# Delta rule: scores kept from the early stage, residual in device memory, seven steps a tile

## The chip, the cores and the metric

One core of a Trainium2 chip. The metric is the device time of one execution in microseconds (us); lower is better. TensorE (PE) multiplies matrices, VectorE (DVE), ScalarE (ACT) and GpSimd (POOL) work element by element, SyncE (SP) issues the transfers. Each engine takes its own instructions strictly in order and waits on semaphores.

## What is computed

Three blocks over 512 tokens of width 1024, each with a gated feed-forward part. The change lies in the third block's gated delta rule, eight heads of 128 by 128, and in what stands around it:

```python
def gated_delta_rule_chunked(q, k, v, g, beta):
    """S_t = exp(g_t)(I - b_t k_t k_t^T) S_{t-1} + b_t k_t v_t^T ; o_t = S_t^T q_t."""
    ...
    gamma = jnp.exp(jnp.where(tri, G[..., :, None] - G[..., None, :], -jnp.inf))
    kb = kc * bc[..., None]
    A = jnp.where(strict, jnp.einsum("bnhid,bnhjd->bnhij", kb, kc) * gamma, 0.0)
    T = lax.linalg.triangular_solve(A + eye, jnp.broadcast_to(eye, A.shape),
                                    left_side=True, lower=True)
    ...
    def step(state, inp):
        u_i, w_i, qg_i, kd_i, att_i, dl_i = inp
        v_new = u_i - jnp.einsum("bhcd,bhde->bhce", w_i, state)
        o = jnp.einsum("bhcd,bhde->bhce", qg_i, state) + jnp.einsum("bhij,bhje->bhie", att_i, v_new)
        state = state * dl_i[..., None, None] + jnp.einsum("bhcd,bhce->bhde", kd_i, v_new)
        return state, o
```

The output then goes through a norm, gates, the product with `w_out` (out2) and a residual sum with the block's input.

## The kernel before

All weights come as 333 units of 512 KB through a ring of six slots (`ring`); SP loads unit u once u-5 units are done. ScalarE rounds each unit to `whi` (L1130), VectorE takes the rest to `wlo` (L1789), and TensorE makes three products per pair (L382 to L384). Both splits run three units ahead.

The third block starts at unit `small2`; unit `dq` 0 is five units later. `XT`, the residual by tokens, lies in `arena` columns 0 to 7 from the norm before (`layered`, L1893) to the sum after out2 (L1842).

*Early stage*, in the units `gqkv` 17 to 21: for each of four tiles of 128 tokens and two groups g of four heads, TensorE spreads decays and beta, VectorE makes beta-scaled keys, TensorE the key products `akk`, and VectorE multiplies their four 32x32 diagonal blocks by the decay into `diag` (L2381). VectorE inverts all these blocks by substitution (L2368, L2370) beside the units `gatea`; the two last transposes (L2422, L2423) end it (`inverted`).

*Delta stage*, from 1679.98 us: `gdn_order` interleaves the two groups, group 1 `LAG` steps behind group 0, and every engine walks the same list of (tile c, group g, part). A tile has nine parts:

- 0: decays `gb` (L961, L962), beta spread `bb` and exp spread `ge` on TensorE; `gam` and `eg` on ScalarE; scaled keys `kb` on VectorE (L2462)
- 1: key products `kk`, value transposes `vt`; scores `at` = -`kk` x `gam` (L2466); ScalarE scales the values (`vb`, L1660); GpSimd makes `kbg` = `kb` x `eg` (L1768)
- 2 to 5: the 128x128 inverse from 32x32 blocks: x5, y5, x6, y6, each a product of TensorE that ScalarE or VectorE copies (x5, x6, y6 on ScalarE, t6 and y5 on VectorE, L2472 to L2474); beside them mean square of the last tile (`ms`, L1006), q products `kq`, key transposes `kt` (L1065), decayed query `eg` (`qg`, L2489)
- 6: `ks` = `kbg` x state; VectorE subtracts it from the values (`r`, L2494) and makes `kd` (L2499)
- 7: new values `vn`; ScalarE copies them into the buffer of `kb`
- 8: `o` (L1100, L1102) and the state product `s`; VectorE norms `o` (L2513) and updates the state (L2518)

GpSimd copies the inverse blocks of a tile into `u`, `t5` and `t6` in part 0 (L1760, L1763), after the tile before has made its new values, and adds the finished tile into the mix (L1773) in part 5. `claim(b)` makes TensorE wait until the last reader of bank b is done; group g uses banks 4g to 4g+3. Before the stage GpSimd clears these buffers with four memsets (L1747, L1748), and VectorE and ScalarE wait for them (`cleared`). In the last tile four pairs of out2 products on `whi` fill TensorE's waits.

## Time and profile before

| | us |
|---|---|
| median of 3 runs | 2209.91 |
| lowest, highest | 2207.5, 2213.14 |
| span of the profiled execution | 2206.0 |
| TensorE busy in it | 2151.8 (98%) |
| VectorE, ScalarE, GpSimd busy | 1299.3, 916.9, 91.5 |

The page gives the profiled execution's span, from its first to its last instruction; its own device time isn't listed apart. Busy time counts an engine's instructions, not its waits; a matmul's end is modelled, so the distance of two starts says more than the length. In a row of the order of time, a bracket gives the idle time before it and what ended it. Operations named L956 are all small products of the delta rule, told apart by shape and place.

### The profile page before, as it was taken

The numbers are of one execution on the slowest core, as the hardware profiler recorded it, in microseconds if no ns is written. First come the engines' busy times: TensorE is split into PE (matmuls) and PEld (weight loads), VectorE is DVE, ScalarE is ACT, GpSimd is POOL, SyncE is SP. The second block draws the span as 40 slices with busy tenths as digits, with TensorE's granted clock in tenths as the row PEclk, the third lists the DMA queues.
The fourth block names the chain that finished last, engine by engine and source line by source line (L and its number), as shares of the span: only waits on it lengthen the run. The fifth ranks groups of instructions, "written<-read, shape, count | busy, mean of one in ns | idle before, by whom it ended". The sixth has DMA issues, their size and how long they took to land.

```text
span 2206.0 us, 26933 instructions
## 1 busy us (share of the span) xinstructions
PE 2151.8 (98%) x10736; PEld 1744.8 (79%) x10736; DVE 1299.3 (59%) x1986; ACT 916.9 (42%) x1549; POOL 91.5 (4%) x123
## 2 busy tenths in 40 slices
...
GB/s 199 94 58 77 67 87 96 96 96 115 98 75 105 67 29 124 97 100 99 116 96 77 96 67 96 77 23 93 77 78 57 1 39 92 99 96 96 115 96 76
DMA packets 50667, 189.82 MB, mean 86 GB/s; under 512 B 5616, under 2 KB 5616, under 8 KB 49776
## 3 DMA queue, kind: packets, MB, share of 16 engines
...
## 4 chain that ended last, share of the span: by engine, by line
PE 89%; DVE 6%; ACT 2%; issue 1%; DMA 1%; POOL 0%; DVEq 0%; ACTq 0%; POOLq 0%
PE bank L382 26%; PE bank L384 26%; PE bank L383 26%; PE bank L956 2%; PE bank L682 1%; DMA ring<-stream 1%; DVE small L1815 1%; PE bank L512 1%; PE bank L660 1%; DVE arena L1842 1%; ACT whi L1130 1%; PE bank L597 0%; DVE arena L1932 0%; PE bank L671 0%; DVE arena L1861 0%
## 5 line engine op out<-in xcount | busy, mean ns | idle before, releaser
L382 PE MATMUL bank<-xs,whi 128*128 128x512 f32 (+2 forms) x1992 | 773.1, 388 | 10.2 <-DVE xs L2148 7.4
L384 PE MATMUL bank<-xs,wlo 128*128 128x512 f32 (+2 forms) x1992 | 753.4, 378 | 0.0
L383 PE MATMUL bank<-xs,whi 128*128 128x512 f32 (+2 forms) x1992 | 752.9, 378 | 0.0
L1789 DVE TENSOR_TENSOR wlo<-ring,whi 128x1024 fp32r<-128x1024 f32 x333 | 416.3, 1251 | 296.6 <-ACT whi L1130 296.2
L1130 ACT ACTIVATE whi<-ring 128x1024 fp32r<-128x1024 f32 x333 | 350.4, 1054 | 262.8 <-DMA ring<-stream 262.8
L382 PEld LDWEIGHTS bank<-xs,whi 128*128 128x128 f32 x1992 | 377.5, 190 | 93.3 <-issue 9.5
L384 PEld LDWEIGHTS bank<-xs,wlo 128*128 128x128 f32 x1992 | 376.8, 189 | 69.3
L383 PEld LDWEIGHTS bank<-xs,whi 128*128 128x128 f32 x1992 | 377.6, 190 | 68.0 <-issue 2.9
L382 PE MATMUL bank<-whi,xs 128*128 128x512 f32 (+1 forms) x808 | 315.2, 390 | 3.5 <-issue 2.0
L384 PE MATMUL bank<-whi,xs 128*128 128x512 f32 (+1 forms) x808 | 311.9, 386 | 0.0
L383 PE MATMUL bank<-wlo,xs 128*128 128x512 f32 (+1 forms) x808 | 311.8, 386 | 0.0
L1433 ACT ACTIVATE arena<-bank,par 128x512 f32<-128x512 f32 x132 | 103.0, 780 | 433.2 <-PE bank L384 433.2
L2091 DVE SCALAR_TENSOR_TENSOR arena<-bank,par,arena 128x511 f32<-128x511 f32 x132 | 98.9, 749 | 286.1 <-ACT arena L1433 286.1
L382 PEld LDWEIGHTS bank<-whi,xs 128*128 128x128 f32 x808 | 152.1, 188 | 38.2 <-issue 5.6
L384 PEld LDWEIGHTS bank<-whi,xs 128*128 128x128 f32 x808 | 152.0, 188 | 30.4
L383 PEld LDWEIGHTS bank<-wlo,xs 128*128 128x128 f32 x808 | 152.2, 188 | 29.9 <-issue 0.5
L2093 DVE SCALAR_TENSOR_TENSOR arena<-bank,par,arena 128x510 f32<-128x510 f32 x132 | 98.9, 749 | 4.7
L1932 DVE SCALAR_TENSOR_TENSOR arena<-bank,par,arena 128x511 f32<-128x511 f32 (+2 forms) x96 | 71.8, 748 | 45.6 <-ACT arena L1596 35.1
L1727 POOL TENSOR_TENSOR arena<-arena 128x512 f32<-128x512 f32 x32 | 52.2, 1668 | 492.0 <-PE bank L512 306.3
L1596 ACT ACTIVATE arena<-bank,par 128x512 f32<-128x512 f32 x24 | 16.5, 687 | 86.0 <-PE bank L384 86.0
L1949 DVE TENSOR_REDUCE small<-bank 128x1 f32<-128x128 f32 (+3 forms) x64 | 31.2, 487 | 34.3 <-PE bank L662 26.5
L2097 DVE TENSOR_TENSOR arena<-arena 128x512 f32<-128x512 f32 x66 | 48.4, 733 | 3.1 <-ACT arena L1436 1.0
...
## 6 DMA issues: line engine op xcount, KB each, us to landing
ring<-stream SPq DMA_DIRECT2D x333, 512.0 KB, 3.6
...
arena<-xt SPq DMA_DIRECT2D x4, 512.0 KB, 6.7
arena<-xn SPq DMA_DIRECT2D x1, 2048.0 KB, 7.9
out<-arena SPq DMA_DIRECT2D x4, 512.0 KB, 2.6
con<-consts SPq DMA_DIRECT2D x1, 744.0 KB, 11.8
arena<-brow SPq DMA_DIRECT2D x1, 512.0 KB, 12.3
...
```

Of the source, the lines that this page charges most:

```text
L382: nc.tensor.matmul(out, ah, bh, start=first, stop=False)
L383: nc.tensor.matmul(out, ah, bl, start=False, stop=False)
L384: return nc.tensor.matmul(out, al, bh, start=False, stop=last)
L956: m = nc.tensor.matmul(tile(b)[0:rows, hh, 0:n], l(hh), r(hh), start=True, stop=True)
L1130: A(whi[:, v % SLOTS, :], ring[:, v % SLOTS, :], ACT.Copy).then_inc(whi_done, 1)
L1433: A(acc[:, s, :], bank_of(up, j)[:], ACT.Identity, bias=col(cols, 4 * j + 3), scale=col(cols, 4 * j + 2)).then_inc(scalar_out, scalar_at.n ...
L1727: nc.gpsimd.tensor_tensor(XT[:, tt, h], XT[:, tt, h], GB[:, i, h], op).then_inc(gpsimd_out, gpsimd_at.next("gained" if i == 0 else "shifte ...
L1789: V.tensor_tensor(wlo[:, v % SLOTS, :], ring[:, v % SLOTS, :], whi[:, v % SLOTS, :], ALU.subtract).then_inc(wlo_done, 1)
L1932: STT(dst[:, shift:], u[:, 0:SEQ - shift], w, dst[:, shift:], ALU.mult, ALU.add).then_inc(vector_out, vector_at.next())
L2091: STT(acc[:, s, 1:], u[:, 0:SEQ - 1], col(cols, 4 * j + 1), acc[:, s, 1:], ALU.mult, ALU.add).then_inc(vector_out, vector_at.next())
L2093: STT(acc[:, s, 2:], u[:, 0:SEQ - 2], col(cols, 4 * j), acc[:, s, 2:], ALU.mult, ALU.add).then_inc(vector_out, vector_at.next("conv", l, j))
L2097: V.tensor_tensor(hid[:, p, :], sg[:, p % 2, :], acc[:, s, :], ALU.mult).then_inc(vector_out, vector_at.next("hidden", l, p))
```

## The change

The early stage keeps its decayed key products whole (`scores`, negated, all eight in `arena` columns 0 to 7), and GpSimd copies the diagonal blocks from them. The residual goes out to device memory (`kept`) ahead of the load of unit `dq` 0 and comes back ahead of the load of unit out2+6. In the delta stage `bb`, `kb`, `kk`, `at` and `kbg` are gone: x5 and x6 read `scores`, `ks` multiplies the plain keys, and `r` adds it times a negated column of beta times the decay, head by head. `t5`, `t6` and `u` are double and GpSimd places a tile's blocks a tile ahead, so there are eight memsets. A tile has seven parts, group 1 runs three behind.

```diff
@@ -183,6 +185,13 @@
...
+    if u == FIRST["dq"]:
+        sp.wait_ge(vector_out, vector_at.find("layered", TILES - 1))
+        sp.dma_start(kept, arena[:, 0:8, :]).then_inc(kept_sem, 16)
+    if u == FIRST["out2"] + SLOTS:
+        sp.wait_ge(kept_sem, 16)
+        sp.wait_ge(tensor_out, tensor_at.find("x6", (TILES - 1, 1)))
+        sp.dma_start(arena[:, 0:8, :], kept).then_inc(xn_sem, 16)
@@ -229,13 +238,17 @@
...
-G |= dict(zip(("at", "u", "kbg", "kd", "vb", "qq"), (heads(scratch[:, 8 * g + i, :]) for i in range(6))))
...
+G |= dict(zip(("kd", "vb", "qq"), (heads(scratch[:, 8 * g + 3 + i, :]) for i in range(3))))
+G["u"] = [heads(scratch[:, 8 * g + i, :]) for i in range(2)]
+pairs, more = scratch[:, 8 * g + 6:8 * g + 8, :].rearrange("p a n -> p (a n)"), scratch[:, 8 * g + 2, :]
+G["pairs"], G["more"] = pairs, more
+quarter = [pairs[:, 256 * i:256 * (i + 1)].rearrange("p (h n) -> p h n", h=4) for i in range(4)]
+half = [more[:, 256 * i:256 * (i + 1)].rearrange("p (h n) -> p h n", h=4) for i in range(2)]
+G["t6"], G["x5"], G["x6"], G["t5"] = [quarter[0], half[0]], quarter[1], quarter[2], [quarter[3], half[1]]
...
-LAG, STEPS = 4, 9
+LAG, STEPS = 3, 7
+scores = [heads(arena[:, i, :]) for i in range(2 * TILES)]
@@ -1010,85 +1023,71 @@
...
+        u, t5, t6 = G["u"][c % 2], G["t5"][c % 2], G["t6"][c % 2]
         if part == 0:
...
-            four(b + 1, lambda hh: spread_rows(2, 4 * g + hh), lambda hh: parts(2, 1)[0:72, cs]).then_inc(tensor_out, tensor_at.next("bb", t))
...
-        elif part == 1:
...
-            four(b + 1, lambda hh: gk[:, 4 * g + hh, cs], lambda hh: G["kb"][:, hh, :]).then_inc(tensor_out, tensor_at.next("kk", t))
...
+                m = nc.tensor.transpose(tile(b + 1)[:, hh, :], gv[:, 4 * g + hh, cs], ident)
...
-        elif part == 2:
...
-        elif part == 3:
...
+        elif part == 1:
...
+            pe.wait_ge(gpsimd_out, gpsimd_at.find("t5", t))
+            at = scores[2 * c + g]
+            four(b, lambda hh: at[:, hh, BLOCK:], lambda hh: t5[:, hh, :], 3 * BLOCK, 64).then_inc(tensor_out, tensor_at.next("x5", t))
...
+        elif part == 2:
+            claim(b)
+            pe.wait_ge(gpsimd_out, gpsimd_at.find("placed", t))
+            four(b, lambda hh: u[:, hh, BLOCK:], lambda hh: G["x5"][:, hh, :], 3 * BLOCK, 64).then_inc(tensor_out, tensor_at.next("y5", t))
...
+            if c:
+                mean_square(c - 1, g)
+            if c < TILES - 1:
+                claim(b + 1)
+                for hh in range(4):
+                    m = nc.tensor.transpose(tile(b + 1)[:, hh, :], gk[:, 4 * g + hh, cs], ident)
+                m.then_inc(tensor_out, tensor_at.next("kt", t))
...
+        elif part == 3:
+            claim(b)
+            pe.wait_ge(vector_out, vector_at.find("t6", t))
+            at = scores[2 * c + g]
+            four(b, lambda hh: at[:, hh, 64:P], lambda hh: t6[:, hh, :], 64, 64).then_inc(tensor_out, tensor_at.next("x6", t))
...
         elif part == 4:
...
-        elif part == 5:
...
-        elif part == 6:
+            four(b, lambda hh: G["x6"][:, hh, :], lambda hh: u[:, hh, 64:P], 64, 64).then_inc(tensor_out, tensor_at.next("y6", t))
...
-                pe.wait_ge(gpsimd_out, gpsimd_at.find("kbg", t))
...
-                four(b + 3, lambda hh: G["kbg"][:, hh, :], lambda hh: state[:, g, hh, :]).then_inc(tensor_out, tensor_at.next("ks", t))
+                four(b + 3, lambda hh: gk[:, 4 * g + hh, cs], lambda hh: state[:, g, hh, :]).then_inc(tensor_out, tensor_at.next("ks", t))
...
+        elif part == 5:
+            claim(b)
+            if c:
+                pe.wait_ge(vector_out, vector_at.find("r", t))
+            else:
+                pe.wait_ge(scalar_out, scalar_at.find("vb", t))
+            four(b, lambda hh: u[:, hh, :], lambda hh: G["vb"][:, hh, :]).then_inc(tensor_out, tensor_at.next("vn", t))
...
-        elif part == 7:
@@ -1107,6 +1106,10 @@
...
+            if t == (TILES - 1, 1):
+                for j in (2, 3):
+                    for half in (0, 1):
+                        out2_part.high(j, 0, half)
@@ -1649,45 +1652,43 @@
...
+        u = G["u"][c % 2]
...
+            act.wait_ge(tensor_out, tensor_at.find("x5", t))
+            A(G["x5"][32:64, :, 0:32], tile(b)[0:32, :, 0:32], ACT.Copy).then_inc(scalar_out, scalar_at.next())
+            A(G["x5"][96:128, :, 32:64], tile(b)[64:96, :, 32:64], ACT.Copy).then_inc(scalar_out, scalar_at.next("x5", t))
...
+                A(G["vb"][:, hh, :], tile(b + 1)[:, hh, :], ACT.Copy, scale=gate_column(3, c, g, hh)).then_inc(scalar_out, scalar_at.next("vb", t))
+        elif part == 3:
...
+            if c:
+                inverse_root(c - 1, g)
...
+        elif part == 4:
+            act.wait_ge(tensor_out, tensor_at.find("y6", t))
+            A(u[0:64, :, 64:128], tile(b)[0:64, :, 0:64], ACT.Copy).then_inc(scalar_out, scalar_at.next("y6", t))
...
+        elif part == 5:
...
+                inverse_root(TILES - 1, 0)
...
+            if t in out2_splits:
+                split_units(out2_splits[t])
+        elif part == 6:
@@ -1742,30 +1743,43 @@
...
+for i in range(2 * TILES):
+    pool.wait_ge(vector_out, vector_at.find("score", i))
+    for b in range(4):
+        q = slice(b * BLOCK, (b + 1) * BLOCK)
+        nc.gpsimd.tensor_copy(diag[q, 4 * i:4 * i + 4, :], scores[i][q, :, q]).then_inc(gpsimd_out, gpsimd_at.next("diag", i))
...
-    nc.gpsimd.memset(G["u"], 0.0).then_inc(gpsimd_out, gpsimd_at.next())
-    nc.gpsimd.memset(G["pairs"], 0.0).then_inc(gpsimd_out, gpsimd_at.next("cleared"))
+    nc.gpsimd.memset(G["pairs"], 0.0).then_inc(gpsimd_out, gpsimd_at.next())
+    nc.gpsimd.memset(G["u"][0], 0.0).then_inc(gpsimd_out, gpsimd_at.next())
+for G in gdn_work:
+    nc.gpsimd.memset(G["more"], 0.0).then_inc(gpsimd_out, gpsimd_at.next())
+    nc.gpsimd.memset(G["u"][1], 0.0).then_inc(gpsimd_out, gpsimd_at.next("cleared"))
...
+
+def place(c, g):
+
+    t, G = (c, g), gdn_work[g]
+    m = slice(c * 8 + 4 * g, c * 8 + 4 * g + 4)
+    pool.wait_ge(gpsimd_out, gpsimd_at.n)
+    if c >= 2:
+        pool.wait_ge(tensor_out, tensor_at.find("vn", (c - 2, g)))
+    for dst, b, x in (("t5", 0, 0), ("t5", 2, 1)):
+        q = slice(b * BLOCK, (b + 1) * BLOCK)
+        nc.gpsimd.tensor_copy(G[dst][c % 2][q, :, BLOCK * x:BLOCK * (x + 1)], lower_diag[q, m, :]).then_inc(gpsimd_out, gpsimd_at.next("t5", t))
+    for b in range(4):
+        q = slice(b * BLOCK, (b + 1) * BLOCK)
+        nc.gpsimd.tensor_copy(G["u"][c % 2][q, :, q], upper_diag[q, m, :]).then_inc(gpsimd_out, gpsimd_at.next())
+    for dst, b, x in (("t6", 0, 0), ("t6", 1, 1)):
+        q = slice(b * BLOCK, (b + 1) * BLOCK)
+        nc.gpsimd.tensor_copy(G[dst][c % 2][q, :, BLOCK * x:BLOCK * (x + 1)], lower_diag[q, m, :]).then_inc(gpsimd_out, gpsimd_at.next("placed", t))
+
+place(0, 0)
+place(0, 1)
...
-        nc.gpsimd.tensor_tensor(G["kbg"], G["kb"], G["eg"], ALU.mult).then_inc(gpsimd_out, gpsimd_at.next("kbg", t))
+    if part == 1 and c < TILES - 1:
+        place(c + 1, g)
@@ -2308,6 +2322,9 @@
...
+    dve.wait_ge(vector_out, vector_at.n)
+    src = bank[4][:, 0:160].rearrange("p (c x) -> p c x", c=TILES)[:, :, 8:16]
+    V.tensor_scalar(small[:, 0:160].rearrange("p (c x) -> p c x", c=TILES)[:, :, 8:16], src, -1.0, None, ALU.mult).then_inc(vector_out, vector_at.next("gate2", "cols"))
@@ -2367,7 +2384,7 @@
...
-            V.tensor_tensor(inverse[:, w:BLOCK, 0:w], inverse[:, w:BLOCK, 0:w], step, ALU.subtract).then_inc(vector_out, vector_at.next("solved", j))
+            V.tensor_tensor(inverse[:, w:BLOCK, 0:w], inverse[:, w:BLOCK, 0:w], step, ALU.add).then_inc(vector_out, vector_at.next("solved", j))
@@ -2376,9 +2393,9 @@
...
-                    V.tensor_tensor(diag[q, 4 * i:4 * i + 4, :], tile(4 + g)[q, :, q], early_decay[g][q, :, q], ALU.mult).then_inc(vector_out, vector_at.next("adiag", i))
+                if i == 0:
+                    dve.wait_ge(kept_sem, 16)
+                STT(scores[i], tile(4 + g), -1.0, early_decay[g], ALU.mult, ALU.mult).then_inc(vector_out, vector_at.next("score", i))
@@ -2405,6 +2422,7 @@
...
+            dve.wait_ge(gpsimd_out, gpsimd_at.find("diag", 2 * TILES - 1))
@@ -2457,56 +2475,49 @@
...
+        u, t6 = G["u"][c % 2], G["t6"][c % 2]
...
-            V.tensor_tensor(G["kb"], gk[:, 4 * g:4 * g + 4, cs], tile(b + 1), ALU.mult).then_inc(vector_out, vector_at.next("kb", t))
...
-            STT(G["at"], tile(b + 1), -1.0, G["gam"], ALU.mult, ALU.mult).then_inc(vector_out, vector_at.next("at", t))
...
+        elif part == 2:
...
+            V.tensor_copy(t6[32:64, :, 0:32], tile(b)[0:32, :, 0:32]).then_inc(vector_out, vector_at.next("t6", t))
+            V.transpose(u[0:32, :, 32:64], tile(b)[0:32, :, 0:32]).then_inc(vector_out, vector_at.next())
+            V.transpose(u[64:96, :, 96:128], tile(b)[64:96, :, 32:64]).then_inc(vector_out, vector_at.next("y5", t))
...
+            dve.wait_ge(scalar_out, scalar_at.find("gam", t))
...
+        elif part == 3:
...
+        elif part == 4:
...
+                for hh in range(4):
+                    n = c * 40 + 8 + 4 * g + hh
+                    STT(G["vb"][:, hh, :], tile(b + 3)[:, hh, :], small[:, n:n + 1], G["vb"][:, hh, :], ALU.mult, ALU.add).then_inc(vector_out, vector_at.next("r", t))
+                scaled(c - 1, g)
...
+                V.tensor_tensor(G["kd"], tile(b + 1), gate_columns(2, c, g), ALU.mult).then_inc(vector_out, vector_at.next("kd", t))
+            if t == (TILES - 1, 1):
+                square_sums(TILES - 1, 0)
+        elif part == 5:
...
+        elif part == 6:
...
+                dve.wait_ge(tensor_out, tensor_at.find("vn", t))
+                dve.wait_ge(vector_out, vector_at.find("scaled", (c - 1, g)))
+                tile_low(0)
@@ -2525,7 +2536,7 @@
...
+    token_norm("out2", "rms2", 1.0, "root", lambda: dve.wait_ge(xn_sem, 32))
```

TensorE's order in the stage, from the beta spread of tile 2, group 0 (banks 0 to 3; group 1 has 4 to 7), before:

```order
L956 MATMUL bank1<-arena 128x128 x4
L956 MATMUL bank2<-arena 128x128 x4
L956 MATMUL bank5<-scratch 64x64 x4
L1065 MATMUL bank6<-con,arena 128x128 x4
L956 MATMUL bank1<-arena 128x128 x4
L1031 MATMUL bank2<-con,arena 128x128 x4
L956 MATMUL bank7<-arena,scratch 128x128 x4
L956 MATMUL bank1<-scratch 96x64 x4
L1006 MATMUL bank3<-scratch,inv128 128x512
L956 MATMUL bank4<-scratch 128x128 x4
L956 MATMUL bank0<-scratch 96x64 x4
L956 MATMUL bank2<-arena 128x128 x4
```

In turn: `bb`, `ge`, the other group's y6 and `kt`, then `kk`, `vt`, the other group's `ks`, x5, `ms`, the other group's `vn`, y5, `kq`. The same place now, from `ge` on:

```order
L969 MATMUL bank2<-arena 128x128 x4
L1037 MATMUL bank1<-con,arena 128x128 x4
L969 MATMUL bank4<-scratch 64x64 x4
L969 MATMUL bank7<-arena 128x128 x4
L969 MATMUL bank0<-scratch,arena 96x64 x4
L969 MATMUL bank2<-arena 128x128 x4
L969 MATMUL bank4<-scratch 128x128 x4
L969 MATMUL bank0<-scratch 96x64 x4
L1019 MATMUL bank3<-scratch,inv128 128x512
L1060 MATMUL bank1<-con,arena 128x128 x4
```

`bb` and `kk` are gone; `vt` (L1037) has moved ahead of the other group's y6, whose `ks` now follows it directly and reads the plain keys; x5 reads the scores in `arena`; `kt` (L1060) has come into the step of y5.

VectorE's order from the norm of `o` to the key scaling, before, where a tile of group 0 ends (bank1 holds its `o`, bank2 its state product):

```order
L2513 SCALAR_TENSOR_TENSOR arena<-bank1,small,arena 128x4x128
L2518 SCALAR_TENSOR_TENSOR arena<-arena,small,bank2 128x128 x4
L2478 TENSOR_TENSOR arena<-bank6,arena 128x512
L2443 TENSOR_TENSOR arena<-arena,scratch 128x4x128
L2462 TENSOR_TENSOR arena<-arena,bank1 128x512
L2485 COPY small<-arena 128x4
L2489 TENSOR_TENSOR arena<-arena 128x512
L2466 SCALAR_TENSOR_TENSOR scratch<-bank1,arena 128x512
L2437 SCALAR_TENSOR_TENSOR scratch<-scratch 128x512
L2494 TENSOR_TENSOR scratch<-scratch,bank7 128x512
L2499 TENSOR_TENSOR scratch<-bank6,small 128x512
```

and now:

```order
L2524 SCALAR_TENSOR_TENSOR arena<-bank1,small,arena 128x4x128
L2529 SCALAR_TENSOR_TENSOR arena<-arena,small,bank2 128x128 x4
L2493 COPY small<-arena 128x4
L2495 TENSOR_TENSOR arena<-arena 128x512
L2455 SCALAR_TENSOR_TENSOR scratch<-scratch 128x512
L2502 SCALAR_TENSOR_TENSOR scratch<-bank7,small,scratch 128x128 x4
L2461 TENSOR_TENSOR arena<-arena,scratch 128x4x128
L2508 TENSOR_TENSOR scratch<-bank5,small 128x512
L1803 TENSOR_TENSOR wlo<-ring,whi 128x1024
L2485 COPY scratch<-bank0 32x4x32
```

`kb` (L2462) and `at` (L2466) are gone, the query product stands ahead of the square sums, and the residual (L2494, now L2502) is four pieces. The split (L1803) that stands behind the key scaling is in three of the tiles only.

SP's order around the third block now, where before 139 ring loads stood in a row:

```order
L198 DMA arena<-gains 128x2048
L200 DMA ring<-stream 128x1024 x27
L190 DMA kept<-arena 128x4096
L200 DMA ring<-stream 128x1024 x66
L194 DMA arena<-kept 128x4096
L200 DMA ring<-stream 128x1024 x46
L198 DMA arena<-gains 128x2048
```

The store stands ahead of 66 ring loads, the load back ahead of 46.

## Rows read from the trace of the kernel before

**Rows 1.** The page's busy time, share and instructions.

```profile
PE 2151.8 (98%) x10736; PEld 1744.8 (79%) x10736; DVE 1299.3 (59%) x1986; ACT 916.9 (42%) x1549; POOL 91.5 (4%) x123
```

**Rows 2.** Stretches: length, busy PE, PEld, DVE, ACT, POOL, clock, DMA, GB/s.

```profile
1679.98:1701.99 22.01, 17.64 (x150) 15.88 (x149) 10.41 (x18) 11.34 (x30) 9.63 (x28) 0.84 0.09 25
1701.99:1713.10 11.11, 10.41 (x99) 9.21 (x98) 7.63 (x16) 7.78 (x19) 4.12 (x9) 1.00 0.01 1
1739.50:1752.82 13.32, 12.23 (x116) 11.02 (x115) 9.58 (x17) 6.84 (x18) 4.82 (x10) 1.00 0.00 1
1766.13:1792.76 26.63, 23.47 (x180) 19.55 (x179) 18.27 (x29) 14.07 (x29) 4.12 (x3) 1.00 0.00 1
1684.00:1692.00 8.00, 6.85 (x41) 6.13 (x42) 1.98 (x5) 2.52 (x9) 3.83 (x14) 0.59 0.01 4
1605.00:1614.00 9.00, 9.00 (x69) 7.69 (x67) 7.16 (x16) 3.70 (x10) 0.00 (x0) 1.00 0.18 60
```

**Rows 3.** TensorE's order of time in one half tile: start, length, line, operands.

```profile
1739.50 0.68 PE L956 MATMUL bank<-scratch 128*64 128x64 f32 x8
...
1740.59 0.61 PE L956 MATMUL bank<-arena 72*128 72x128 bf16 x8
...
1741.13 0.68 PE L956 MATMUL bank<-scratch 128*64 128x64 f32 x8
...
1742.67 1.13 PE L956 MATMUL bank<-arena 128*128 128x128 f32 x8 [0.28 <-DVE arena L2462]
...
1743.64 0.60 PE L1031 MATMUL bank<-con,arena 128*128 128x128 f32 x4
...
1745.94 0.86 PE L956 MATMUL bank<-scratch 128*96 128x64 f32 x8 [0.81 <-DVE scratch L2466]
```

**Rows 4.** VectorE's order of time, norm before the block, early and delta stage.

```profile
1227.05 1.28 DVE L1893 SCALAR_TENSOR_TENSOR arena<-arena,small 128x1024 f32<-128x1024 f32 x1
...
1596.25 2.51 DVE L2381 TENSOR_TENSOR arena<-bank,arena 32x128 f32<-32x128 f32 x8
...
1694.13 0.69 DVE L2489 TENSOR_TENSOR arena<-arena 128x512 f32<-128x512 f32 x1
...
1708.88 1.23 DVE L1789 TENSOR_TENSOR wlo<-ring,whi 128x1024 fp32r<-128x1024 f32 x1 [1.18 <-ACT whi L1130]
...
1739.61 1.12 DVE L2518 SCALAR_TENSOR_TENSOR arena<-arena,small,bank 128x128 f32<-128x128 f32 x4
...
1743.47 1.77 DVE L2489 TENSOR_TENSOR arena<-arena 128x512 f32<-128x512 f32 x1
```

**Rows 5.** GpSimd's order of time in the delta stage.

```profile
1682.03 0.95 POOL L1748 MEMSET scratch<- 128x1024 f32 x1
...
1683.15 1.32 POOL L1760 COPY scratch<-arena 32x128 f32<-32x128 f32 x4 [0.17 <-DVE arena L2426]
...
1709.40 1.89 POOL L1760 COPY scratch<-arena 32x128 f32<-32x128 f32 x4 [3.07 <-PE bank L956]
...
1743.42 1.27 POOL L1768 TENSOR_TENSOR scratch<-arena 128x512 f32<-128x512 f32 x1
```

**Rows 6.** ScalarE's order of time, third block's opening and delta stage.

```profile
1239.82 1.99 ACT L1130 ACTIVATE whi<-ring 128x1024 fp32r<-128x1024 f32 x2
...
1683.22 1.14 ACT L1591 ACTIVATE arena<-bank,small 128x128 f32<-128x128 f32 x4
...
1749.85 0.63 ACT L1648 ACTIVATE scratch<-scratch 128x512 f32<-128x512 f32 x1
```

**Rows 7.** TensorE's order of time at the delta stage's start.

```profile
1683.85 1.13 PE L956 MATMUL bank<-arena 128*128 128x128 f32 x8 [2.53 <-DVE arena L2462]
...
1685.99 1.51 PE L956 MATMUL bank<-scratch 128*96 128x64 f32 x8 [0.41 <-POOL scratch L1763]
```

**Rows 8.** DMA issues: operands, KB each, median us to landing.

```profile
arena<-xn SPq DMA_DIRECT2D x1, 2048.0 KB, 7.9
out<-arena SPq DMA_DIRECT2D x4, 512.0 KB, 2.6
```

122 lines of the change are left out of this document (12 added, 110 removed).

## The prediction

> **What bounds the kernel now.** I read the page first, then the stretches of the delta stage, then each engine's order of time in one half tile of it. On the page TensorE is busy 98% of the span at full clock [rows 1]: nearly everywhere only fewer matmuls help. The stretches of the delta stage (1679.98 to 1792.76 us, 112.8 us) are where TensorE is not full: 22.0 us hold 17.6 busy, at a mean clock of 0.84, then 11.1 hold 10.4, four halves hold 12.2 each in 13.3 (one row stands for four; the first of them is 13.1 long), and the end of 26.6 holds 23.5 [rows 2]. Idle time is 12 us, busy time 100.
>
> One half tile is the time from the end of one group's state product to the end of the other's. In TensorE's order of time [rows 3] it idles twice in it: 0.28 us for the scaled keys (L2462) and 0.81 for the negated scores (L2466). Both come late because VectorE's queue is held: the query product (L2489) takes 1.77 us [rows 4] beside GpSimd's key product of 1.27 us [rows 5]. The first query product, with GpSimd idle, took 0.69 [rows 4].
>
> **What is removed.** Per tile and group TensorE loses the beta spread (four bf16 matmuls, half of the 0.54 us from 1740.59 to 1741.13, so 0.27) and the key products (1742.67 to 1743.64, 0.97) [rows 3]: 1.24 us, busy 12.23 to 11.0. VectorE loses the scaled keys and the scores (0.6 each by starts), and GpSimd the 1.27 us key product. The residual now takes four 128x128 operations, which in the state update take 1.12 us [rows 4], for one of 0.67. The two steps fewer (seven, not nine) and the removed operations delete both waits of TensorE.
>
> **The new half tile, walked.** T is the end of a group's state product s (in the row, 1739.50). An operation's length on TensorE is the distance to the next start in the same stretch as [rows 3]; those of the others are the lengths in [rows 4] and [rows 6].
>
> - TensorE opens with x6 of the other group, to T+0.61, and the decays (0.48), to 1.09. The exp spread then claims the bank that the state update reads. That update ends 1.23 after s (1740.73 against 1739.50) [rows 3, 4]; with 0.1 for the semaphore the spread starts at 1.33, a wait of 0.24, and ends at 1.60. Value transposes (0.43) to 2.03, y6 (0.61) to 2.64, the state's key product (0.97) to 3.61.
> - ScalarE meanwhile: the square of o and the x6 copy, to T+1.16; the root of 1.34 (its second half is 0.63 [rows 6]), which now stands ahead of the decays; four exponentials at distances of 0.25: T+3.6. They read the bank that x5 claims, so x5 starts at 3.65.
> - TensorE goes on: x5 (0.70) to 4.4, kq (0.94) to 5.3, new values (0.85) to 6.2, y5 (0.69) to 6.9, mean square (0.91) to 7.8, key transposes (0.43) to 8.2, o (1.79) to 10.0, s (0.99) to 11.0.
> - What else could be late: the residual (3.61 and 0.15 and 1.1, so 4.9; wanted at 5.3), the y6 copy on ScalarE (4.5; wanted at 5.3), the copied new values (7.3; wanted at 8.2), t6 on VectorE (7.4; wanted at 11.0).
>
> So a half is 11.0 by the walk, 11.3 by busy time and the two waits of 0.3; I take **11.3**. Three halves hold a split of out2 weights (1.07 us on ScalarE, then 1.21 on VectorE), which now stands between the new values and the t6 copy. There t6 is ready at 10.4, the scaled query scores at 11.1, the normed o at 11.8, and the state update ends 1.9 after s instead of 1.2: I charge 0.65 us for each.
>
> - Five halves (11.1, 13.1, 3 times 13.3 before): 9.6 for the first, which has no state product, then 11.3 each; saved 1.5+1.8+3x2.0 = 9.3, less 2.0: **7.3**.
> - **Start.** The scores are there, but x5 needs GpSimd and ScalarE. Four more memsets of half the size (0.47 each) follow the four that end at 1682.98, less 0.1 of overlap each side: all done at 1684.9, after the inverse (1682.4); two copies of 0.33 follow: 1685.6 [rows 5]. ScalarE waits for all memsets too, so its four exponentials of 1.14 us [rows 6] end at 1686.0, not 1684.4. So x5 starts at 1686.1, against 1685.99 [rows 7]: nothing gained. Then x5 and kq at half clock 1.4+2.0, y5 and key transposes 2.3, x6 and the other group's first step 2.5, y6 0.6, its x5 and kq 1.7, new values and y5 1.6, transposes and the wait for the copied values 0.55, o and s 1.95, together 14.6: 1700.7 for 1701.99. Saved **1.3**.
> - **End.** From the last state product to the first whole out2 product was 26.63 us [rows 2]. Walked in the same way: y6 at 10.95, second residual at 13.75 (idle 1.35; ScalarE's root and split of 1.04 also hold the y6 copy to 13.6), new values 14.8, mean square 16.0 after 0.3 idle, four half products 17.8, o 19.6, four more 21.4, eight low products 23.2, mean square 24.1. Saved **2.5**.
>
> Sum 11.1.
>
> **Edits costed at nothing, and their cover.** (a) Scores early: VectorE replaces eight 32x128 products (2.51 us [rows 4]) by two 128x512 (1.2) in each of four units, and is busy 7.16 of 9.0 us there while TensorE is full [rows 2]. GpSimd's 32 copies of 0.33 go beside it. Beside a split (1708.88) four such copies took 1.89 us instead of 1.32, and the split stayed at 1.23 [rows 4, 5]. The Trainium skill, "SBUF — State Buffer", section "Who interferes with whom", says the shared port pair is locked for a whole instruction and a VectorE operation with two SBUF inputs waits for a GpSimd read; the row shows the copies as the loser, the query product as the other case. By the rule each split could lose one copy, 0.33, which the idle 1.84 still hides: the sum is the same by both at TensorE; without that idle it would be 1.3 us less. The transpose of the scores (1634.3) comes some 8 us after the last copy would end. (b) Store: SP waits for the last layered tile (end 1228.33 [rows 4]) before it may ask for unit dq. The nearest rows for 2 MB are the token load, 7.9 us, and 0.5 MB out in 2.6 [rows 8]. Landing about 1236.5, then the unit about 1240; ScalarE takes it up at 1240.8, second of the two of 1239.82 [rows 6]. TensorE needs it split at 1255.9, so 14 us of cover are left. Bounds: 0, and case 4. (c) Load back: issued at the last x6, 10 us after T, wanted at 1816 in before's time; 8 us of transfer, 40 of cover. Later ring loads wait for out2 units as before; the 1.5 us stall on them stays.
>
> **The cases.** Below 0.3% (6.6 us) a measurement can't tell a change.
>
> 1. *As summed*: 11.1 us less, 0.62; its own range 7 to 13.5.
> 2. *Better, 0.13*: the splits and the first bank claim cost nothing and halves take 11.0: 2.0 and 1.2 more, 14.3 less, 2195.6.
> 3. *VectorE and GpSimd collide in each half, 0.16.* GpSimd still adds 1.27 us and places 2.6 us a half, and VectorE's sums, scaling and query product read SBUF twice. For: 0.69 became 1.77 [rows 4]. Against: the products that waited in that row ran beside 1.27 us operations, and the placing copies ran with no such stretch. If one hit of 1.07 lies on the way to the residual or t6 in each of five halves, 5.4 us go: 5.7 less, 2204, the same within noise. The rule of the Trainium skill given above is this rival's.
> 4. *The store blocks the ring, 0.05, slower.* The unit dq stands behind 2 MB in SP's queue, and ScalarE and VectorE wait for it in order. The Trainium skill, "DMA: Bandwidth & Descriptors", section "Two DMAs through the same engine are not ordered", says descriptors of one queue start in order. It decides from a store of 24 us (87 GB/s) on; at 50 GB/s it takes 42, the unit lands at 1274 and TensorE stands 21 us: 10 us slower, 2220. Against: 0.5 MB written in 2.6 us.
> 5. *It gives nothing, 0.04*: a new idle stretch at the start keeps the half clock for longer. TensorE now idles 1682.5 to 1686.1; before it idled 2.53 and then 0.41 [rows 7], and the clock averaged 0.59 over the 8 us from 1684 [rows 2], most of them at 1.2 GHz. Seven more us at that level cost 3.5; thrice that would be needed.
>
> **The number.** The span is 2206.0 and the median of the runs 2209.9; the profiled execution's own time stands nowhere beside its span, so I take the same 3.9 us on top: 2206.0+3.9-11.1 = 2198.8, said as **2199**. Range 2193 to 2206: case 1, 2 and 3 with 1.5 us of spread between runs leave out a tenth. Faster: cases 1 and 2 and a fifth of 3, 0.78; same 0.17; slower 0.05.
>
> **What would show it.** Right: half tiles of 11.0 to 11.5 us (three with 0.6 more), no idle time of TensorE on VectorE's scores, the query product at 0.7, a wait of 0.2 at the exp spread, x5 of the first tile within 0.5 us of where it was, and a ScalarE that never waits for unit dq. Wrong: halves of 12 or more with waits for the residual or t6 (3), idle TensorE about 1256 (4), a clock under 1 after 1693 (5), or TensorE busy time that fell by less than 9 us.

## The result and the profile after

| kernel | median us | lowest, highest | runs |
|---|---|---|---|
| before | 2207.82 | 2207.34, 2213.14 | 6 |
| after | 2196.56 | 2193.95, 2199.62 | 6 |

The ratio is 0.9942, with a 95% interval of 0.9929 to 0.9954: 12.8 us less by the ratio, 11.3 by the medians, faster by more than the 0.3% that can be told from no change. A later set of six runs of the same kernel gave 2199.46 and a ratio of 0.9954 [0.9939, 0.9969]. The forecast was 2199.0 us and a gain of 11.1.

The page of the kernel after, to be read against [rows 1]:

```profile
span 2193.5 us, 26724 instructions
PE 2142.8 (98%) x10640; PEld 1735.3 (79%) x10640; DVE 1278.9 (58%) x1965; ACT 917.3 (42%) x1549; POOL 98.4 (4%) x153
```

The span is 12.5 us shorter. TensorE is busy 9.0 us less, 3.5 us of its idle time are gone too, and VectorE has lost 20 us. The difference lies in the delta stage. Its stretches after (columns as in [rows 2]):

```profile
1681.33:1701.32 19.99, 15.17 (x129) 13.72 (x129) 8.19 (x15) 11.25 (x30) 16.49 (x48) 0.83 0.10 27
1701.32:1710.39 9.07, 9.04 (x87) 7.95 (x86) 4.98 (x13) 6.48 (x17) 3.25 (x9) 1.00 0.01 3
1710.39:1722.81 12.42, 11.14 (x104) 9.82 (x103) 8.85 (x22) 7.69 (x19) 4.65 (x9) 1.00 0.01 1
1722.81:1734.40 11.59, 11.08 (x104) 9.82 (x103) 8.29 (x21) 7.69 (x19) 4.46 (x9) 1.00 0.01 2
1734.40:1746.03 11.63, 11.07 (x103) 9.81 (x102) 7.88 (x20) 6.74 (x18) 1.27 (x1) 1.00 0.01 1
1746.03:1756.55 10.52, 10.48 (x99) 9.41 (x98) 7.26 (x18) 6.74 (x18) 1.27 (x1) 1.00 0.00 0
1756.55:1780.96 24.41, 22.47 (x168) 18.85 (x168) 16.76 (x32) 15.20 (x31) 2.85 (x2) 1.00 0.24 88
```

Against [rows 2]: the start 20.0 us for 22.0, the five halves 55.2 for 64.1, the end 24.4 for 26.6. That is 13.1 us, and the span shows 12.5: the stage begins 1.4 us later (first decays at 1681.38, against 1679.98), and what follows it is 0.7 us shorter. The later start is no cost of the change, for in a second profile of the same kernel, taken with its later set, the first decays are at 1679.99. Between 1260 and 1300 us, where TensorE has no idle time, the granted clock is 0.91 in this profile and 0.96 in the second and in that of before.

One half tile in TensorE's order of time, the one that answers to [rows 3]:

```profile
1734.40 0.68 PE L969 MATMUL bank<-scratch,arena 128*64 128x64 f32 x8
1736.20 0.40 PE L969 MATMUL bank<-arena 72*128 72x128 bf16 x4 [0.56 <-DVE arena L2529]
1736.44 0.61 PE L1037 MATMUL bank<-con,arena 128*128 128x128 f32 x4
1736.97 0.68 PE L969 MATMUL bank<-scratch 128*64 128x64 f32 x8
1737.58 1.16 PE L969 MATMUL bank<-arena 128*128 128x128 f32 x8
1738.69 0.89 PE L969 MATMUL bank<-scratch,arena 128*96 128x64 f32 x8
...
1745.05 1.06 PE L969 MATMUL bank<-arena,scratch 128*128 128x128 f32 x8
1746.03 0.68 PE L969 MATMUL bank<-scratch,arena 128*64 128x64 f32 x8
```

From one x6 (1734.40) to the next the rows mark one idle time, before the exp spread, which waits for VectorE's state update (L2529). The waits for the scaled keys and for the scores are gone. VectorE at the same place, against [rows 4]:

```profile
1731.47 1.27 DVE L1803 TENSOR_TENSOR wlo<-ring,whi 128x1024 fp32r<-128x1024 f32 x1 [1.81 <-ACT whi L1133]
1732.77 0.28 DVE L2485 COPY scratch<-bank 32x128 f32<-32x128 f32 x1
...
1735.03 1.11 DVE L2529 SCALAR_TENSOR_TENSOR arena<-arena,small,bank 128x128 f32<-128x128 f32 x4
1736.06 0.17 DVE L2493 COPY small<-arena 128x4 f32<-128x4 f32 x1
1736.26 0.69 DVE L2495 TENSOR_TENSOR arena<-arena 128x512 f32<-128x512 f32 x1
...
1738.78 1.13 DVE L2502 SCALAR_TENSOR_TENSOR scratch<-bank,small,scratch 128x128 f32<-128x128 f32 x4 [1.23 <-PE bank L969]
```

The query product (L2495) takes 0.69 us, not 1.77. The split (L1803) stands ahead of t6 (L2485), and through it the state update ends 1.7 us after the state product (1736.06, against 1734.40).

### The profile page after: what moved, and what is told of

Its sections match the earlier page's. It is cut to its first block, busy times and chain, and to the rows that moved or that the text cites. A ratio compares the mean times of both kernels' runs of the same rounds, so it can differ in the third digit from the quotient of the medians.

```text
span 2193.5 us, 26724 instructions
## 1 busy us (share of the span) xinstructions
PE 2142.8 (98%) x10640; PEld 1735.3 (79%) x10640; DVE 1278.9 (58%) x1965; ACT 917.3 (42%) x1549; POOL 98.4 (4%) x153
## 4 chain that ended last, share of the span: by engine, by line
PE 89%; DVE 5%; ACT 3%; issue 1%; DMA 1%; POOL 0%; ACTq 0%; DVEq 0%; POOLq 0%
PE bank L395 26%; PE bank L397 26%; PE bank L396 26%; PE bank L969 2%; PE bank L695 1%; DMA ring<-stream 1%; DVE small L1829 1%; PE bank L525 1%; PE bank L673 1%; DVE arena L1856 1%; ACT whi L1133 1%; PE bank L610 1%; DVE arena L1946 0%; PE bank L684 0%; DVE arena L1875 0%
## 5 line engine op out<-in xcount | busy, mean ns | idle before, releaser
L395 PE MATMUL bank<-xs,whi 128*128 128x512 f32 (+2 forms) x1992 | 771.4, 387 | 10.3 <-DVE xs L2162 7.5
L1803 DVE TENSOR_TENSOR wlo<-ring,whi 128x1024 fp32r<-128x1024 f32 x333 | 415.7, 1250 | 302.7 <-ACT whi L1133 302.3
L1133 ACT ACTIVATE whi<-ring 128x1024 fp32r<-128x1024 f32 x333 | 350.8, 1055 | 263.0 <-DMA ring<-stream 262.9
L1963 DVE TENSOR_REDUCE small<-bank 128x1 f32<-128x128 f32 (+3 forms) x64 | 31.3, 488 | 34.3 <-PE bank L675 26.6
## 6 DMA issues: line engine op xcount, KB each, us to landing
con<-consts SPq DMA_DIRECT2D x1, 744.0 KB, 11.3
```

What stands on the lines that cost most here:

```text
L395: nc.tensor.matmul(out, ah, bh, start=first, stop=False)
L1133: A(whi[:, v % SLOTS, :], ring[:, v % SLOTS, :], ACT.Copy).then_inc(whi_done, 1)
L1803: V.tensor_tensor(wlo[:, v % SLOTS, :], ring[:, v % SLOTS, :], whi[:, v % SLOTS, :], ALU.subtract).then_inc(wlo_done, 1)
```

## Experiments

Kernels of one group ran on one chip and share the runs of the kernel before.

| kernel | median us | runs | ratio to before, 95% interval |
|---|---|---|---|
| first group: before | 2208.99 | 10 | |
| no store, no load back | 2198.53 | 4 | 0.9945 [0.993, 0.996] |
| products back | 2203.7 | 7 | 0.9972 [0.9961, 0.9983] |
| second buffers cleared later | 2191.06 | 4 | 0.9912 [0.989, 0.9934] |
| split after the scores' decay | 2194.24 | 4 | 0.9933 [0.9916, 0.995] |
| second group: before | 2207.86 | 15 | |
| before with plain keys | 2205.66 | 10 | 0.9982 [0.9971, 0.9993] |
| blocks placed in their tile | 2199.36 | 4 | 0.9963 [0.9949, 0.9977] |
| tiny placing copies | 2196.43 | 4 | 0.995 [0.9936, 0.9963] |
| both edits | 2191.89 | 5 | 0.9931 [0.9919, 0.9944] |
| third group: before | 2209.85 | 17 | |
| six stores | 2210.54 | 8 | 1.0001 [0.9987, 1.0014] |
| after | 2199.46 | 6 | 0.9954 [0.9939, 0.9969] |
| second buffers cleared later | 2195.79 | 6 | 0.9943 [0.9924, 0.9963] |
| both edits | 2191.21 | 6 | 0.9917 [0.9902, 0.9933] |

**Do the transfers cost anything?** The store, the load back and the waits on them are left out:

```diff
-                if u == FIRST["dq"]:
-                    sp.wait_ge(vector_out, vector_at.find("layered", TILES - 1))
-                    sp.dma_start(kept, arena[:, 0:8, :]).then_inc(kept_sem, 16)
-                if u == FIRST["out2"] + SLOTS:
...
```

> The changed kernel without the store of the residual and without its load back. The residual sum after out2 therefore adds the kept scores in place of the residual; only that part of the computation differs, and the work of every compute engine is the same. My theory: both transfers are covered (in the changed kernel's trace the store lands 7.2 us and the load 8.0 us after their issue, and ScalarE does not wait for unit dq 0), so the time is that of the changed kernel, 2196.6 us within 0.3%, ratio to before 0.992 to 0.997, and TensorE's idle time at the third block's opening is the same to 0.1 us. Rival: the store holds back the ring loads behind it or the load back disturbs the out2 loads; then 2 to 6 us less, ratio 0.990 to 0.993.

The ratio is 0.9945, against 0.9942 for after: the transfers cost nothing that was seen. In after ScalarE takes unit dq up without a wait (the second of the two L1133; L1533 is the copy ahead of them, as before):

```profile
1240.70 0.59 ACT L1533 ACTIVATE arena<-bank 64x512 f32<-64x512 f32 x1
1241.20 2.00 ACT L1133 ACTIVATE whi<-ring 128x1024 fp32r<-128x1024 f32 x2
```

and the transfers took what their nearest rows said [rows 8] (KB each, median us to landing):

```profile
kept<-arena SPq DMA_DIRECT2D x1, 2048.0 KB, 7.2
arena<-kept SPq DMA_DIRECT2D x1, 2048.0 KB, 8.0
```

**How near was the rival on the slower side?** The residual stored six times over:

```diff
-                    sp.dma_start(kept, arena[:, 0:8, :]).then_inc(kept_sem, 16)
+                    for copy in range(6):
+                        sp.dma_start(kept[copy], arena[:, 0:8, :]).then_inc(kept_sem, 16)
```

> The kernel after with the residual stored six times over, each to a place of its own, ahead of the load of unit dq; the last is loaded back. This is the rival of the prediction on the slower side, made larger: six times 7.2 us is some 43 us of store. If the load stands behind the stores, unit dq lands about 1273 us, ScalarE's rounding of it waits more than 25 us, TensorE stands still for about 20 us from about 1256, and the kernel takes 15 to 22 us more than after (some 2212 to 2218). If loads and stores share the engines without order, the unit lands at about half the rate, before 1245, and the kernel stays within 3 us of after.

It is 11.1 us over after (2210.54 against 2199.46 in the same group), and level with before. First ScalarE's order of time, then its waits and TensorE's between 1225 and 1300 us, then the stretch from 1230 (columns as in [rows 2]):

```profile
1264.28 1.06 ACT L1134 ACTIVATE whi<-ring 128x1024 fp32r<-128x1024 f32 x1 [21.82 <-DMA ring<-stream]
```

```profile
ACT whi L1134 <- DMA ring<-stream: 21.8, 1, 21.8
...
PE bank L396 <- ACT arena L1166: 9.7, 1, 9.7
```

```profile
1230.00:1260.00 30.00, 27.51 (x179) 24.19 (x177) 9.10 (x21) 9.53 (x26) 0.96 (x1) 1.00 0.99 413
```

So the load does stand behind the stores, and the mechanism of case 4 is real. The expectation (15 to 22) was too high, because six stores in a row move faster than one alone: 413 GB/s with the DMA engines 99% busy, so that ScalarE could take unit dq up 34.3 us after the first store was issued (1229.96), and not after 43. TensorE stood still for 9.7 us, from 1257.5 on, until ScalarE had made the first of its copies that stand behind this unit (L1166). One store leaves all of it hidden.

**What are the removed matmuls worth?** The beta spread and the key products are made again, unread, into the bank that the value transposes use:

```diff
                         claim(b + 1)
+                        four(b + 1, lambda hh: spread_rows(2, 4 * g + hh), lambda hh: parts(2, 1)[0:72, cs])
+                        four(b + 1, lambda hh: gk[:, 4 * g + hh, cs], lambda hh: gk[:, 4 * g + hh, cs])
```

> The changed kernel with four bf16 and four f32 matmuls put back into each tile and group on TensorE (the beta spread and key products by key, into the bank that the value transposes overwrite; nobody reads them). Nothing is left out of the computation. My theory: a half tile is bound by TensorE, so each of the eight pieces of 1.22 us comes back almost whole, less the wait of 0.2 to 0.5 us at the exp spread, which ends before the pieces: seven or eight times 1.1 to 1.25, 8 to 10 us more than the changed kernel, near 2205.5 us, ratio to before 0.998 to 1.0, half tiles of 12.2 to 12.8 us. Rival: the gain came from the shorter chain of steps and waits; then the pieces fill waits and the time rises by 0 to 3 us, half tiles stay at 11.6.

The gain was 11.3 and 10.4 us by the medians of after's two sets (12.8 and 10.2 by the ratios); here it is 5.3 (6.2). So the matmuls carry 4 to 7 us, less than the 8 to 10 expected; "no store, no load back" of the same group, which is level with after, is 5.2 us faster. By the trace it is 7.1 us, against the later profile of after, whose start has the same clock: 1.3 in the start, 4.7 in the five halves (10.3, 13.0, 12.5, 12.5 and 11.6 from x6 to x6) and 1.1 in the end. The five halves had some 6 us of matmuls added (1.17 each by the starts). The rest of it lies where TensorE would otherwise wait: in the last half with a split the wait at the exp spread falls from 0.56 to 0.44 us, and some 0.1 us ahead of x5, for the exponentials, is gone.

**What was VectorE's hold worth?** This starts from the kernel before. Only `kbg` goes, and the waits for it; the nine parts, the beta spread and the key products stay:

```diff
-                            pe.wait_ge(gpsimd_out, gpsimd_at.find("kbg", t))
...
-                    nc.gpsimd.tensor_tensor(G["kbg"], G["kb"], G["eg"], ALU.mult).then_inc(gpsimd_out, gpsimd_at.next("kbg", t))
...
-                        if c:
-                            dve.wait_ge(gpsimd_out, gpsimd_at.find("kbg", t))
...
-four(b + 3, lambda hh: G["kbg"][:, hh, :], ...
+four(b + 3, lambda hh: gk[:, 4 * g + hh, cs], ...
...
-V.tensor_tensor(G["vb"], G["vb"], tile(b + 3), ALU.subtract)
+for hh in range(4): STT(G["vb"][:, hh, :], tile(b + 3)[:, hh, :], small[:, n:n + 1], G["vb"][:, hh, :], ALU.mult, ALU.add)
```

> The kernel before with one edit: the product of the decayed state reads the plain keys, GpSimd no longer makes the key product, and the residual adds the product times a negated column of beta times the decay in four 128x128 operations. Everything else is as before, the beta spread, the key products and the nine parts too. My theory (before the change GpSimd's key product held VectorE's query product, and with it the negated scores that TensorE waited for): the query product falls from 1.77 to 0.7 us, TensorE's 0.81 us wait for the scores goes, a half tile takes 12.3 to 12.6 us for 13.3, and the kernel takes 4 to 6 us less than before. Rival A (the wait has another cause, the number of VectorE's operations): the query product shortens, the residual's four pieces take 0.45 us more, the halves stay within 0.3 us of 13.3 and the kernel within 2 us of before. Rival B (GpSimd's product was not what stretched the query product): it stays at 1.7 us.

The ratio gives 4.0 us (1.5 to 6.4) and the medians 2.2, where 4 to 6 were expected. The trace is plainer: from one tile's decays to the next group's, the four full halves take 49.5 us for 53.0, so 3.6 less, and TensorE's wait for the scores is gone from them. VectorE's and GpSimd's orders of time in one of them:

```profile
1758.25 0.93 DVE L2482 COPY small<-arena 128x4 f32<-128x4 f32 x1
1759.21 0.69 DVE L2484 TENSOR_TENSOR arena<-arena 128x512 f32<-128x512 f32 x1
```

```profile
1757.88 1.27 POOL L1767 TENSOR_TENSOR arena<-arena 128x512 f32<-128x512 f32 x1 [3.96 <-DVE arena L2440]
```

GpSimd's mixing product ends at 1759.15, and only then do VectorE's copy of 128x4 (0.93 us for 0.17 alone) and the query product come through. In the kernel before the same copy was held by the mixing product, and the query product by the key product behind it:

```profile
1755.76 0.92 DVE L2485 COPY small<-arena 128x4 f32<-128x4 f32 x1
1756.79 1.77 DVE L2489 TENSOR_TENSOR arena<-arena 128x512 f32<-128x512 f32 x1
```

```profile
1755.39 1.27 POOL L1773 TENSOR_TENSOR arena<-arena 128x512 f32<-128x512 f32 x1 [3.95 <-DVE arena L2443]
1756.74 1.27 POOL L1768 TENSOR_TENSOR scratch<-arena 128x512 f32<-128x512 f32 x1
```

The key product ends at 1758.01, and the query product 0.55 us later. The program's own wait for `kbg` ahead of the query product, which this edit takes out too, is no rival: it is for the key product of the same tile, and that had ended half a tile earlier (the one at 1743.42 in [rows 5]); the one beside the query product is the other group's.

The two experiments together also say what nine steps made into seven are worth by themselves. With the products back, the seven steps take 12.5 to 13.0 us for a full half; with plain keys, the nine steps take 12.3 to 12.5. So no gain of the shorter list shows beside the two named; no run changes it alone.

**Is placing a tile ahead worth anything?** Placed in the tile's own part 0:

```diff
-                if c >= 2:
-                    pool.wait_ge(tensor_out, tensor_at.find("vn", (c - 2, g)))
+                if c >= 1:
+                    pool.wait_ge(tensor_out, tensor_at.find("vn", (c - 1, g)))
...
-                if part == 1 and c < TILES - 1:
-                    place(c + 1, g)
+                if part == 0 and c >= 1:
+                    place(c, g)
```

> The kernel after, with GpSimd placing the inverse blocks in the tile they belong to (in its part 0, once the tile before has made its new values) and not a tile ahead. My theory: a tile has seven parts and a half tile some 11 us, the new values of the tile before are done about 3 us before x5 starts in the next tile, and four copies for t5 take 0.7 of them, so placing ahead is worth 0 to 0.5 us a half at most: the kernel takes 0 to 2 us more than after (2196 to 2199). Rival (placing ahead is what lets the tile be seven parts): x5 waits for GpSimd by 1 us or more in each of six half tiles, 6 us or more altogether, 2202 and above.

All distances from decays to decays of the next group, from the third on, are those of after to 0.02 us (9.23, 12.24, 11.58, 11.62, 10.52), and there is no wait for GpSimd. The median, 2199.36, lies between the two of after. Placing ahead and the double buffers of the inverse blocks gain nothing that was seen.

**Does GpSimd's placing cost VectorE time?** One column of each block is copied for tiles 1 to 3:

```diff
+                wide = BLOCK if c < 1 else 1
...
-G["u"][c % 2][q, :, q], upper_diag[q, m, :]
+G["u"][c % 2][q, :, b * BLOCK:b * BLOCK + wide], upper_diag[q, m, 0:wide]
```

> The kernel after, with GpSimd's placing copies for tiles 1 to 3 cut to one column of each 32x32 block, so that they take a few hundredths of a us each and hardly touch SBUF; the tiles 1 to 3 then work with incomplete inverse blocks (part of the computation is left out). My theory (beside VectorE the copies are the ones that are stretched, and VectorE loses nothing that TensorE waits for): half tiles within 0.1 us of after's 12.4, 11.6, 11.6 and 10.5, the waits at the exp spread stay 0.5 to 0.9, the kernel within 1.5 us of after. Rival (the copies cost VectorE time on the way to the state update, the residual or t6): the waits at the exp spread fall to 0.3 or less and the halves by 0.3 to 0.6 us each, 2 to 3 us less than after.

Hardly anything changes at TensorE: the halves take 12.24, 11.58, 11.57 and 10.52 us, the waits at the exp spread are 0.93, 0.50 and 0.50 (the third half and its wait are 0.06 shorter than in after, the others the same). The copies of 32x4 at the split, GpSimd and then VectorE:

```profile
1731.74 1.91 POOL L1774 COPY scratch<-arena 32x4 f32<-32x4 f32 x4
1733.71 0.42 POOL L1777 COPY scratch<-arena 32x4 f32<-32x4 f32 x2
```

```profile
1732.37 1.23 DVE L1804 TENSOR_TENSOR wlo<-ring,whi 128x1024 fp32r<-128x1024 f32 x1 [1.80 <-ACT whi L1133]
```

Two free ones take 0.42, so four would take 0.84; they took 1.91, while the split kept 1.23. Of full size, in after, they took 2.21 for 1.33. So 0.9 and 1.1 us were waited beside a split of 1.23, whatever the copies' size; that it was one copy is read from that, since the row holds all four. The forecast's reading of [rows 4, 5], that the copies lose beside a split and the split does not, holds.

**Where do the waits that are left come from?** Two edits of after. In the first the second buffers are cleared behind the first placing:

```diff
             for G in gdn_work:
                 nc.gpsimd.memset(G["pairs"], 0.0)...
-                nc.gpsimd.memset(G["u"][0], 0.0).then_inc(gpsimd_out, gpsimd_at.next())
-            for G in gdn_work:
-                nc.gpsimd.memset(G["more"], 0.0)...
-                nc.gpsimd.memset(G["u"][1], 0.0).then_inc(gpsimd_out, gpsimd_at.next("cleared"))
+                nc.gpsimd.memset(G["u"][0], 0.0).then_inc(gpsimd_out, gpsimd_at.next("cleared"))
...
             place(0, 1)
+            for G in gdn_work: (the other two memsets)
```

> The changed kernel with the four memsets of the second buffers moved behind the first two tiles' placing on GpSimd, so that ScalarE and VectorE wait for four memsets and not for eight. My theory: the start of the delta stage hangs on those memsets by way of ScalarE's decay exponentials, which start at 1686.4 after the eighth memset (1686.25) while the activation table is loaded at 1684.6. They can then start at 1684.6 or 1684.7, 1.7 us sooner; x5 of the first tile follows at 1685.9 or so in place of 1687.6. With less idle time of TensorE the half clock may also last shorter. 1.5 to 3 us less than the changed kernel, 2194 to 2195 us, ratio 0.9929 to 0.9937. Rival: the first steps are bound by the half clock, which stays as long from a fixed time on; then 0 to 0.5 us.

ScalarE, after and then with the edit:

```profile
1686.41 1.14 ACT L1594 ACTIVATE arena<-bank,small 128x128 f32<-128x128 f32 x4 [1.81 <-POOL scratch L1757]
```

```profile
1683.31 1.28 ACT L1642 ACT_TABLE_LOAD   x1
1684.60 1.14 ACT L1594 ACTIVATE arena<-bank,small 128x128 f32<-128x128 f32 x4
```

The exponentials now follow their table load, and x5 starts 4.4 us into the stage instead of 6.2. In the second edit VectorE splits out2's weights behind the decay product (`att`) of the other group:

```diff
-                    elif part == 5:
-                        if t in out2_splits:
-                            split_units(out2_splits[t])
...
                         V.tensor_tensor(G["gam"], tile(b + 2), G["gam"], ALU.mult)...
+                        other = (c, 0) if g else (c - 1, 1)
+                        if other in out2_splits:
+                            split_units(out2_splits[other])
```

> The changed kernel with VectorE's three out2 splits of the delta stage placed behind the query scores (part 2) of the other group, in its idle time before the normed output, and not between the key scaling and the t6 copy. ScalarE's part is where it was. My theory: the split delays t6, scores, norm and state update and with them the exp spread, so the three half tiles that hold one (12.4, 11.6 and 11.6 us in the changed kernel) become 11.0 to 11.2 and the wait of 0.51 and 0.56 us at the exp spread falls to 0.2 to 0.3: 1 to 2 us less than the changed kernel. Rival: the wait at the exp spread is due to the order of operations before the state update itself and stays; then 0 to 0.3 us, or more if the split is now late for the norm.

TensorE's waits at the exp spread are gone from its rows, and the halves that had them take 11.42, 10.96 and 10.97 us for 12.25, 11.59 and 11.63 from x6 to x6. With the 0.17 us ahead of the first of them, which is gone too, that is 2.3 less in the trace, where 1 to 2 were expected. By the medians the gain over before is 14.8 us, where after's two sets have 11.3 and 10.4; the intervals of the ratios overlap. Both edits together:

> The kernel after with two edits together: the second buffers are cleared after the first tile's blocks are placed, and VectorE's split of out2 weights stands behind the decay product of the other group instead of between the new values and the copy of t6. Alone each took 2.3 us out of the delta stage by its trace. My theory (the two waits are at different places and the gains add): x6 of the first tile starts 2.3 us earlier, the three half tiles with a split take 11.0 to 11.4 us for 11.6 to 12.4, together 4 to 4.6 us less than after, 2191 to 2193 us, ratio to before 0.990 to 0.992. Rival (they don't add, since the splits then wait for ScalarE's rounding or out2's start waits for them): no more than 2.5 us under after, ratio 0.993 or above.

16.0 us under before by the medians. This group held no runs of after, so the three kernels ran once more side by side:

> The kernel after once more, unedited, beside the next two on one chip, so that they are compared with it directly. Both theories: 2194 to 2198 us, ratio to before 0.993 to 0.9955.

> The kernel after with the second buffers cleared after the first tile's blocks are placed, once more beside after. If the first look's 5.5 us under after was the 2.3 us of the trace plus the spread of the clock, it is 2 to 3 us under after here. If the shorter stretch at half clock gives more than the wait itself, 4 to 6 us.

> The kernel after with both edits, once more beside after and beside the one edit. If the gains add as the traces of the delta stage say (2.3 and 2.3 us), it is 4 to 6 us under after and 2 to 2.5 us under the one edit. If the second gain goes into a later wait for the low halves of out2's weights, it is level with the one edit.

The first edit is 3.7 us under after by the medians, between its two theories (0.9954 and 0.9943 by the ratios, whose intervals overlap). Both are 8.3 us under after, where 4 to 6 were expected (0.9954 [0.9939, 0.9969] and 0.9917 [0.9902, 0.9933]), and 4.6 under the one edit, where 2 to 2.5 were. So both together are faster than either kernel of the study, 2191.2 us; how much of it belongs to the first edit alone the runs don't separate: its two sets gave 0.9912 and 0.9943.

## Why the prediction was right, point by point

**The sum.** 11.1 us forecast, 11.3 by the medians, 12.8 by the ratio. The stated time was 2.4 us too high, and 2.1 of that is the base: I took 3.9 us between span and time, from the median of three runs. The profiled execution of after took 2195.32 for a span of 2193.5, so 1.8, and the six runs of before have a median of 2207.8, which is 2206.0 and 1.8. That the gain fits to 0.2 us is in part luck: against the later profile of after the halves gave 9.0 for 7.3, the start 0.4 for 1.3 and the end 2.2 for 2.5, and the errors offset each other. The matmuls and the waits that the sum named are those that the runs show.

**Five halves: 7.3 forecast, 8.9 measured.** The walk gave 11.0 and the busy time with waits 11.3; I took the larger. The edit of the split shows a half with all its work and no wait: 10.97 us. So the walk was right, and taking 11.3 cost some 1.2 us. The last half is shorter still, 10.52, because the last tile has no key transposes (0.43), which the sum forgot; the first took 9.07 for 9.6. The charge for a split, 0.65, was exact in two of the three halves (11.6 less 10.97) and short in the first of them, 12.42, where the wait at the exp spread is 0.93, with others of 0.17 ahead of it and 0.19 behind. The exp spread without a split was forecast 1.33 us after the state product and came at 1.29, here from 1746.03:

```profile
1747.32 0.40 PE L969 MATMUL bank<-arena 72*128 72x128 bf16 x4
```

With a split it came at 1.80 (1736.20 against 1734.40); the charge puts it at 1.98.

**Which part of it was which.** Removing VectorE's hold alone gave 3.6 us in the trace, putting the matmuls back took 7.1. The forecast had the first as a wait of TensorE and the second as 1.24 us a half; 3.6 and 7.1 are 10.7 of the 11 to 13 gained. The runs' own times are less sharp (2.2 or 4.0 for the first, 4 to 7 for the second), so the split between them is good to a few us only.

**Start: 1.3 forecast, 2.1 in this profile, 0.4 in another.** x5 was forecast 6.1 us after the stage begins, and came at 6.2 (6.0 before) [rows 7]; GpSimd's eight memsets ended 4.9 us after it, as forecast. What differs is the clock behind it. Two profiles of the same kernel, stretches of 5 us at the same distance from the stage's start, first that of the result, then the later one (columns as in [rows 2]):

```profile
1691.38:1696.38 5.00, 4.75 (x49) 4.02 (x48) 3.06 (x7) 2.17 (x8) 4.24 (x14) 0.84 0.02 3
```

```profile
1689.99:1694.99 5.00, 4.75 (x34) 4.10 (x32) 3.00 (x7) 1.34 (x5) 4.18 (x14) 0.50 0.02 3
```

The same matmuls stand ahead with the same idle times; in the second TensorE is at 1.2 GHz through all of the 5 us, in the first it is back at 2.4 GHz for most of them. From the stage's first decays to those of the second tile it is 20.55 us in the one and 22.21 in the other, and before it was 22.62 (from 1679.98):

```profile
1702.60 0.23 PE L961 MATMUL bank<-arena 72*128 72x128 bf16 x1
```

The profiles of the five experiments that keep after's start (no store, six stores, late split, placed in their tile, tiny copies) have the length of the second to 0.2 us, none that of the first: the short one was seen once in seven. So the gain at the start is 2.1 or 0.4 us by these marks, with the forecast of 1.3 between, and 0.4 is the usual one. Case 5 (the idle time keeps the half clock for longer) is a cost of 1.7 us that was there in six of the seven profiles; it is far from one that takes the whole gain. From x5 to the end of the stretch the forecast's walk had 14.6 us; the one profile shows 13.7, the other 15.4. With the buffers cleared later x5 starts 1.8 us sooner, the clock is back early in all four profiles of that order, and the stretch takes 17.9 to 18.3 us: more than the wait itself against the usual 22.2.

**End: 2.5 forecast, 2.2 measured.** The idle time before the second new values was forecast as 1.35 and is 1.31. What lacks is a wait of 0.48 for the y6 copy, which before was 0.52 and which the walk had hidden. (The second row names ScalarE's L1682, but the program makes the new values wait for the second residual there, which ends within 0.03 us of it: 13.8 us into the end, forecast 13.75.)

```profile
1767.34 0.68 PE L969 MATMUL bank<-scratch 128*64 128x64 f32 x8 [0.48 <-ACT scratch L1670]
...
1770.53 1.13 PE L969 MATMUL bank<-scratch 128*128 128x128 f32 x8 [1.31 <-ACT arena L1682]
```

**The rivals.** Case 3, VectorE against GpSimd in each half: it did not come, since the tiny copies change hardly anything and the query product is at 0.69. The reason differs from the one given. The forecast left it at "no such stretch" for the copies; but GpSimd's arithmetic does hold VectorE, and still adds 1.27 us a half. Beside VectorE it now runs with the key scaling (L2508), which takes one operand from PSUM, and neither is longer than alone:

```profile
1740.61 0.69 DVE L2508 TENSOR_TENSOR scratch<-bank,small 128x512 f32<-128x512 f32 x1
```

```profile
1740.65 1.27 POOL L1787 TENSOR_TENSOR arena<-arena 128x512 f32<-128x512 f32 x1 [6.71 <-DVE arena L2461]
```

It ends at 1741.92, before VectorE has its next work (1742.11). One meeting is left, in the end: beside GpSimd's last mixing product (1771.12 to 1772.70) a VectorE product with both inputs in SBUF (L2473) took 2.10 us, and 1.23 later; no run shows whether that costs time. The rule of the Trainium skill, "SBUF — State Buffer", "Who interferes with whom", fits what was held in both directions: VectorE's products until GpSimd's instruction had ended, GpSimd's copies by 0.9 to 1.1 us beside a split of 1.23. The copy of 128x4 has one SBUF input and was held too. That section of the Trainium skill also says that a copy can take both ports in a 2-port mode and then contends; no run here shows in which mode this one ran. Case 4, the store: the ring load waits as the Trainium skill, "DMA: Bandwidth & Descriptors", "Two DMAs through the same engine are not ordered", says of one queue, shown by the six stores; one store is far from enough. That placing ahead is worth anything was not claimed, and it is not.
